# Strict mask by TensorE, forget rows on ScalarE, lambdas and copies of normed tiles as later steps, both ratios of a differential pair at once

## Time and profile before

| | us |
|---|---|
| median of three runs | 1549.19 |
| the profiled execution | 1553.94 |
| its span, first to last instruction | 1552.0 |
| TensorE busy | 1423.3 (92%) |
| VectorE busy | 904.6 (58%) |
| ScalarE busy | 681.2 (44%) |
| GpSimd busy | 366.7 (24%) |

### The profile page before, as it was taken

The page is one execution under the profiler, slowest core; times in us unless marked ns, Lnnn a source line. Parts: engine busy times, 40 slices in busy tenths (PEclk is TensorE's granted clock), DMA queues, the critical chain, the costliest instruction groups (busy, mean ns, idle before and its releaser), DMA issues.

```text
span 1552.0 us, 21224 instructions
## 1 busy us (share of the span) xinstructions
PE 1423.3 (92%) x8026; PEld 1097.0 (71%) x8026; DVE 904.6 (58%) x1705; ACT 681.2 (44%) x1477; POOL 366.7 (24%) x265
## 2 busy tenths in 40 slices
PE   7999898999989999999998699997999799997997
PEld 7757675877987576767788666665777656664776
DVE  4655437556672554484576565468655466568655
ACT  3544344555233554444552344335444444335443
POOL 2232121245231321222452111410001111310011
PEclk9999999999999999999999799999999899998999
DMA  6412620225333121211263323511213322511211
GB/s 225 109 29 85 158 68 28 62 61 204 109 136 82 29 82 55 82 35 56 67 224 85 93 54 68 116 55 48 93 64 96 82 63 60 116 55 48 96 62 54
DMA packets 191120, 131.72 MB, mean 85 GB/s; under 512 B 91436, under 2 KB 181164, under 8 KB 191020
## 3 DMA queue, kind: packets, MB, share of 16 engines
q1 hardware_dynamic: 179534, 112.29, 26.0%
q10 hardware_dynamic: 11486, 18.09, 3.6%
HBM read 118.03 MB, written 12.32 MB: 84 GB/s over the span
## 4 chain that ended last, share of the span: by engine, by line
PE 68%; DVE 18%; ACT 7%; issue 3%; DMA 2%; ACTq 1%; POOL 0%; DVEq 0%; POOLq 0%
PE pb L1399 18%; PE pb L1400 16%; PE pb L1401 16%; PE pb L1477 5%; PE pb L1421 5%; PE pb L1455 4%; ACT prob L1533 2%; DMA wr<-w_out 2%; ACT wh L1552 2%; ACT tmp L1533 1%; DVE wl L1861 1%; DVE scr L2151 1%; DVE xl L1868 1%; DVE small L2128 1%; PE pb L1439 1%
## 5 line engine op out<-in xcount | busy, mean ns | idle before, releaser
L2296 POOL TENSOR_TENSOR wl<-wr,wh 128x512 fp32r<-128x512 f32 x170 | 236.7, 1392 | 893.8 <-ACT wh L1552 890.1
L1399 PE MATMUL pb<-xh,wl 128*128 128x512 f32 (+1 forms) x832 | 354.0, 425 | 25.1 <-DVE xl L1868 21.9
L1400 PE MATMUL pb<-xl,wh 128*128 128x512 f32 (+1 forms) x832 | 323.6, 389 | 0.0
L1401 PE MATMUL pb<-xh,wh 128*128 128x512 f32 (+1 forms) x832 | 323.2, 388 | 0.0
L1861 DVE TENSOR_TENSOR wl<-wr,wh 128x512 fp32r<-128x512 f32 x200 | 162.9, 815 | 159.3 <-ACT wh L1552 159.0
L1399 PEld LDWEIGHTS pb<-xh,wl 128*128 128x128 f32 x832 | 164.0, 197 | 106.4 <-issue 54.1
L1552 ACT CAST wh<-wr 128x512 fp32r<-128x512 f32 x370 | 211.0, 603 | 50.2 <-PE pb L1401 42.8
L1401 PEld LDWEIGHTS pb<-xh,wh 128*128 128x128 f32 x832 | 163.5, 197 | 32.0
L1400 PEld LDWEIGHTS pb<-xl,wh 128*128 128x128 f32 x832 | 164.8, 198 | 24.3 <-issue 3.8
L1533 ACT ACTIVATE prob<-prob,small 128x512 f32<-128x512 f32 (+3 forms) x128 | 76.2, 597 | 153.0 <-DVE small L2105 143.6
L1455 PE MATMUL pb<-cst,prob 128*128 128x128 f32 x768 | 118.5, 276 | 24.4 <-ACT prob L1533 8.2
(11 more groups left out here) (196 smaller groups left out, 2449.9 us busy)
## 6 DMA issues: line engine op xcount, KB each, us to landing
wr<-w_in SPq DMA_DIRECT2D x39, 1024.0 KB, 5.1
wr<-w_in SPq DMA_DIRECT2D x48, 256.0 KB, 4.6
wr<-w_out SPq DMA_DIRECT2D x10, 1024.0 KB, 5.7
wr<-w_branch SPq DMA_DIRECT2D x48, 128.0 KB, 2.3
x<-prob SPq DMA_DIRECT2D x12, 512.0 KB, 2.6
wr<-w_out SPq DMA_DIRECT2D x48, 128.0 KB, 3.0
wr<-w_mem_kv SPq DMA_DIRECT2D x4, 1024.0 KB, 5.5
prob<-x ACTq DMA_DIRECT2D x2, 2048.0 KB, 10.3
```

The costliest lines, as they stand in the source:

```text
L1399: e.matmul(ps, ll, rh, start=start, stop=False)
L1400: e.matmul(ps, lh, rl, start=False, stop=False)
L1401: t = e.matmul(ps, lh, rh, start=False, stop=stop)
L2296: t = e.tensor_tensor(wl[:, j % 2, c0:c1], wr[:, j % 2, c0:c1], wh[:, j % 2, c0:c1].bitcast(F32), ALU.subtract)
```

## The change

1. The constant `after` (zeros and ones) becomes `strict` (0 and -1e30, 128 columns). `lambdas` also copies it and the identity to two new tiles. `sqk` adds per half one TensorE product of identity and mask to the diagonal block of the logits, after both halves' logits; both halves' logits are marked ready only then. `sticks` loses line 2154 and the mask in its scan.
2. `lambdas` and `spread` stand after the query projection of `sb` instead of before it.
3. `foxrow` is done by ScalarE (`Identity` with scale and bias) instead of VectorE.
4. `normed` keeps only the VectorE part. A step `normhi` with the ScalarE copies and the GpSimd differences is put when the planner's clock is 5000 further, or at the latest where `rest_of` is called: for the queries' group that is directly after `krope`, for the other group in the gate projection that follows.
5. `dmix` does reciprocal and product for both halves in one instruction each, after waiting for both halves' exponentials.

```diff
-    put("after", np.concatenate([np.zeros((P, 384)), c >= p], 1))
+    put("strict", np.where(c >= p, NEG, 0.0))
...
             put("normed", l=l, b=b, tm=tm, tn=tn, dim=dim, grp=grp, gain=gain)
             give(b, tm, tn)
+            ready = now() + 5000
+            for _ in range(40):
+                if now() < ready:
+                    yield
+            put("normhi", l=l, grp=grp)
...
         put("krope", l=l, b=b)
         give(b)
+        rest_of(norm_q)
...
+        rest_of(norm_kv)
         w = wnext("qb")
...
             yield from gate_into(box, "g1", "sb", l)
+            yield from proj_fm("sbq", l, "sb", "q", l, False)
             if l == 0:
                 put("lambdas")
                 put("spread")
-            yield from proj_fm("sbq", l, "sb", "q", l, False)
...
-                    t = e.matmul(bank(b)[:, 0:128 * (hi - lo)], lhs, rhs, start=True, stop=br != "mla")
-                    if br != "mla":
+                    t = e.matmul(bank(b)[:, 0:128 * (hi - lo)], lhs, rhs, start=True, stop=br not in ("mla", "sb"))
+                    if br not in ("mla", "sb"):
+                        t.then_inc(logit.sem, logit.mark(b))
+                if br == "sb":
+                    w.wait_ge(v_fn, v_fn.at("masks"))
+                    for b in s["b"]:
+                        t = e.matmul(bank(b)[:, 128 * i:128 * i + 128], identr[:, :], strict[:, :], start=False, stop=True)
                         t.then_inc(logit.sem, logit.mark(b))
...
-            elif k == "normed":
+            elif k == "normhi":
                 for n in s["grp"]:
                     w.wait_ge(v_fn, v_fn.at(("normed", s["l"], n)))
...
+            elif k == "foxrow":   # in scalar_program, out of vector_program
+                l, h = s["l"], s["h"]
+                w.wait_ge(v_fn, v_fn.at(("foxsum", l)))
+                w.wait_ge(p_fn, p_fn.at(("zeros", l)))
+                fa, fb = CONST_COLS["foxa"][0], CONST_COLS["foxb"][0]
+                p0 = 64 * (1 - h % 2)
+                for dst, n in ((QKV["fox"][0], 0), (QKV["fox"][1], 1 + h)):
+                    t = act(dst[p0:p0 + 36, h, :], fz[:, :], ACT.Identity, cst[0:36, fa + n:fa + n + 1],
+                            cst[0:36, fb + n:fb + n + 1])
+                    t.then_inc(a_copy.sem, a_copy.mark(("foxrow", l, h)))
...
             elif k == "lambdas":
+                w.wait_ge(d_tail, d_tail.at("tail"))
+                e.tensor_copy(identr[:, :], C("ident")).then_inc(v_fn.sem, v_fn.mark())
+                e.tensor_copy(strict[:, :], C("strict")).then_inc(v_fn.sem, v_fn.mark("masks"))
...
             elif k == "dmix":
                 l, i = s["l"], s["i"]
+                first, ratio = (small[:, s["sm"].slot.i, c + i:c + i + 5:4] for c in (8, 24))
+                for use in s["ta"]:
+                    w.wait_ge(a_att, a_att.at(("exp", use)))
+                e.reciprocal(ratio, ratio).then_inc(v_att.sem, v_att.mark())
+                w.wait_ge(v_att, v_att.n)
+                t = e.scalar_tensor_tensor(ratio, ratio, lam[:, l:l + 1], first, ALU.mult, ALU.mult)
+                t.then_inc(v_att.sem, v_att.mark())
+                w.wait_ge(v_att, v_att.n)
                 for half in range(2):
...
-                    m = mask_cols("after", 512 - n, 512)
-                    t = e.tensor_tensor_scan(lo[:, ::-1], x[:, ::-1], m[:, ::-1], 1.0, ALU.mult, ALU.max)
+                    t = e.tensor_tensor_scan(lo[:, ::-1], x[:, ::-1], x[:, ::-1], 1.0, ALU.mult, ALU.bypass)
...
-                    t = e.scalar_tensor_tensor(d[:, dg], mask_cols("after", 384, 512), 1.0, d[:, dg], ALU.is_lt, ALU.mult)
-                    t.then_inc(v_att.sem, v_att.mark())
...
-            elif k == "normed":   # in gpsimd_program
+            elif k == "normhi":
                 l = s["l"]
                 for n in s["grp"]:
                     own()
```

More of the change, by code:

```diff
@@ L1129, in build @@
     fz = sb("fz", [36, S])
+    identr, strict = sb("identr", [P, P], F32R), sb("strict", [P, P], F32R)
     mrh, mrl = sb("mrh", [P, S], F32R), sb("mrl", [P, S], F32R)
@@ L1335, in heads_ready @@
                 if br == "fox":
-                    w.wait_ge(v_fn, v_fn.at(("foxrow", l, 3)))
+                    w.wait_ge(a_copy, a_copy.at(("foxrow", l, 3)))
                 w.wait_ge(v_copy, v_copy.at(("value", l, br, 2)))
@@ L2012, in vector_program @@
                 t.then_inc(v_fn.sem, v_fn.mark(("foxsum", l), ends=(s["e"],)))
[L2013 to L2022, removed]
             elif k == "mergeup":
@@ L2131, in vector_program @@
                 l, i = s["l"], s["i"]
-                for half in range(2):
[L2133 to L2138, removed]
-                    t.then_inc(v_att.sem, v_att.mark())
-                    w.wait_ge(v_att, v_att.n)
-                    t = e.scalar_tensor_tensor(d, tm(use), ratio, d, ALU.mult, ALU.add)
+                first, ratio = (small[:, s["sm"].slot.i, c + i:c + i + 5:4] for c in (8, 24))
[6 more added lines that the diff above has]
+                w.wait_ge(v_att, v_att.n)
+                for half in range(2):
+                    d, p, use = probs(s["e"][half]), s["e"][half], s["ta"][half]
+                    t = e.scalar_tensor_tensor(d, tm(use), sm(s["sm"], 24 + 4 * half + i), d, ALU.mult, ALU.add)
                     t.then_inc(v_att.sem, v_att.mark(("mixed", p), ends=(use,)))
@@ L2146, in vector_program @@
                     w.wait_ge(d_spread, d_spread.at("z"))
-                    x, lo, d, dg = tm(use)[:, 0:n], tmpz[:, 0:n], probs(p)[:, 0:n], slice(n - 128, n)
+                    x, lo, d = tm(use)[:, 0:n], tmpz[:, 0:n], probs(p)[:, 0:n]
                     w.wait_ge(a_att, a_att.at(("keep", use)))
                     w.wait_ge(v_att, v_att.n)
-                    m = mask_cols("after", 512 - n, 512)
-                    t = e.tensor_tensor_scan(lo[:, ::-1], x[:, ::-1], m[:, ::-1], 1.0, ALU.mult, ALU.max)
+                    t = e.tensor_tensor_scan(lo[:, ::-1], x[:, ::-1], x[:, ::-1], 1.0, ALU.mult, ALU.bypass)
                     t.then_inc(v_att.sem, v_att.mark(ends=(use,)))
                     w.wait_ge(a_att, a_att.at(("break", p)))
-                    t = e.scalar_tensor_tensor(d[:, dg], mask_cols("after", 384, 512), 1.0, d[:, dg], ALU.is_lt, ALU.mult)
-                    t.then_inc(v_att.sem, v_att.mark())
                     w.wait_ge(v_att, v_att.n)
```

## The result

The changed kernel takes 1539.18 us (median of 4 runs, 1536.47 to 1541.01) against 1549.34 of before, run on the same chips: ratio 0.9928, 95% interval 0.9911 to 0.9946, so 11 us faster by the ratio and 10.2 by the medians. A second set of 6 runs gave 1539.16 and 0.9937 [0.9918, 0.9956]. The forecast was 1532 (1520 to 1543): the direction and the range held, but the gain is about 10 us and not 17.6.

What follows compares the result with a forecast made beforehand. It took TensorE, busy 92% of the span, as the bound; -10.1 (norms) + 0.2 (move) - 8.9 (stick breaking) + 3.0 (masks) - 1.8 (ratios) = -17.6 from 1549.2 gave 1531.6, predicted as 1532 us, range 1520 to 1543.

Steps and rivals of the forecast that it cites:

- clock terms: Matmuls behind shortened TensorE waits return to full clock: 4.3 us gained at the norms, 3.1 in stick breaking.
- Norms, gaps 5.8: Before `pv` in both layers: TensorE's waits of 3.12 and 3.07 fall to 0.2 each, 5.8 us gained.
- The port's 1.1: Second Newton step at the norms: GpSimd's differences may hold VectorE by 1.1 us per layer; in the range only.
- Move +0.2: `lambdas` and `spread`: ScalarE's blockade only moves, TensorE stands 5.9 us instead of 5.25; sum +0.2.
- Stick breaking, gaps 5.8: VectorE loses masks and `foxrow`, so four TensorE waits per layer shorten: 2.9 us per layer, 5.8 in all.
- the chain scan, clear, product loses its middle, 0.30: VectorE in stick breaking: removing the clear between scan and product shortens the path by 0.30 us each time.
- Masks +3.0: TensorE's 32 added mask products cost 2.2 us after hiding, plus 0.8 for changes of format: +3.0.
- ScalarE's `foxrow` 0: ScalarE's 16 added instructions, 11.6 us, fit into its pauses: cost 0, bounds 0 and +4.
- Rival D: In `sb`, `Identity` for `foxrow` forces function table loads between sigmoids, making the kernel slower: 1576 us; chance 0.03.
- Ratios -1.8: Branch D, `dmix`: joining both halves saves 0.44 us ahead of the waits of 3.51 and 3.09, both layers: -1.8.
- rival A: TensorE's waits shrink but the lower clock stays or falls elsewhere: 1539 us; chance 0.22 together with B.
- B: At the norms, something else becomes what `pv` waits for: 1539 us; chance 0.22 together with rival A.

Runs made afterwards that it cites:

- Mask and forget rows together: Kernel before with the strict mask added by TensorE and `foxrow` done by ScalarE, no other edit: 1546.55 us, ratio 0.9976.
- Norms alone: Kernel before with only the copies and differences of the normed tiles as a later step (`normhi`): 1540.17 us, ratio 0.9944.
- The kernel before with SyncE: Kernel before with the two DMAs of `spread` issued by SyncE instead of ScalarE, at the old place: 1542.64 us, ratio 0.9948.
- forget rows alone: Kernel before with only `foxrow` moved from VectorE to ScalarE: 1545.96 us, ratio 0.9969.
- ratios alone: Kernel before with only `dmix` doing reciprocal and product for both halves at once: 1550.30 us, ratio 1.0000.
- with SyncE: Changed kernel with the two DMAs of `spread` issued by SyncE instead of ScalarE: 1530.43 us, ratio 0.9880 to the kernel before.
- without masks: Changed kernel with SyncE issuing the DMAs of `spread` and VectorE masking the logits as before: 1528.62 us, ratio 0.9853 to the kernel before.

## Why the prediction was right, and where its size was not

**The gap terms held.** Without its clock terms (4.3 for the norms, 3.1 for stick breaking) the sum was -17.6 + 7.4 = -10.2. At equal clock the runs show 9.1 to 10.4. That it fits so well is in part luck, as the terms below were off by up to 1.2 us either way: the traces give 7.0 for the norms, 5.1 for stick breaking, 1.2 for the wait for GpSimd that had no term, 1.0 for the ratios, less 3.5 for the products and 0.5 for the move, together 10.3.

- *Norms, gaps 5.8:* the waits are gone entirely (rest forecast 0.2 each), and a wait of 0.73 before the transposes at 106.67, and its twin in layer 1, fell to 0.32, which no term had: 6.2 + 0.8 = 7.0 in the traces, 5.7 measured at equal clock for this edit alone. The port's 1.1, kept for the range, came as 0.8 and 1.0 (1.50 for 0.67, 1.66 for 0.69) and was hidden.
- *Move +0.2:* the new wait was forecast as 5.9 and is 5.75, ended by ScalarE's copy as said, at 183 and not 190. Measured +1.2 [-1.4, +3.9].
- *Stick breaking, gaps 5.8:* waits of 0.9, 0.7, 0.7, 0.7 were forecast, and are 0.81, 0.91, 0.88, 0.82. They sum to 3.42 per layer for 3.0, so 5.1 in all. The step that failed a little is "the chain scan, clear, product loses its middle, 0.30". The rows below (before, then after) show it: the clear had run in the time that the product must wait for the scan anyway. From one scan to its product it was 0.90, and without the clear it is 0.79: 0.11 is saved, and the wait before 235.23 fell by just that, 1.02 to 0.91. The first wait fell by 0.47, but 0.36 of it is time in which TensorE now computes the pair of mask products instead of standing, and so no gain.

```profile
232.33 0.68 DVE L2151 TENSOR_TENSOR_SCAN scr<-tmp,cst 128x256 f32<-128x256 f32 x1
232.93 0.27 DVE L2154 SCALAR_TENSOR_TENSOR prob<-cst,prob 128x128 f32<-128x128 f32 x1
233.23 0.42 DVE L2157 TENSOR_TENSOR prob<-prob,scr 128x255 f32<-128x255 f32 x1
```
```profile
225.05 0.68 DVE L2167 TENSOR_TENSOR_SCAN scr<-tmp 128x256 f32<-128x256 f32 x1
225.84 0.42 DVE L2171 TENSOR_TENSOR prob<-prob,scr 128x255 f32<-128x255 f32 x1
```

- *Masks +3.0:* 0.22 per step for 16 steps, 3.5 before what is hidden. The products that fall into waits show as shorter waits above, so the whole 3.5 counts here. Mask and forget rows together are 5.1 + 1.2 - 3.5 = 2.8; measured 3.7 [1.1, 6.2] with 0.7 of clock.
- *ScalarE's `foxrow` 0:* 12.2 us of work and no wait behind it. Rival D is out: no table load. The Trainium skill, ScalarE: Activation LUTs, section on table sets, has identity in every set; the rows agree.
- *Ratios -1.8:* waits fell by 1.1 alone and 1.0 in the whole. Per layer the 0.44 comes twice, as forecast, but not both times where forecast. The 3.51 gives 0.45. The `dmix` ahead of the 3.09 gives its 0.44 in the shorter wait before it, which the prediction did not name, and the 3.09 keeps its length: from the start of the logits ahead of both it is 1084.01 - 1078.53 = 5.48 before and 1067.32 - 1062.28 = 5.04 after. So it is not the later half's exponentials that keep the 3.09, as had been expected; the reciprocal of that `dmix` doesn't wait. They take back elsewhere: in four of the eight `dmix` of a layer the reciprocal stands about 0.53 for them, more than the 0.44 saved, once just ahead of the wait that grew from 0.20 to 0.48. Measured 0.0 [-2.2, +2.0].

**The clock terms failed.** The steps "the matmuls of 116 to 121 lose 1.85", "the other `pv` gives back 0.9", "the logits of 259.71 lose 0.75, and those behind them 0.5" are each true of the two traces: those stretches do run at full clock in the changed kernel. What failed is adding them to the time, as if a slow stretch belonged to its wait. The traces show that it doesn't. Norms alone has the waits of 2.35 and 2.36 with the logits at 0.92 and 1.65. The kernel before with SyncE has 2.38 and 2.36, and 0.92 both times. And with forget rows alone and with ratios alone the `pv` of layer 1 takes 1.08 behind a wait of 3.12, and the slow stretch begins only with the matmuls after it. In the changed kernel a new slow stretch stands behind the shorter waits of stick breaking in layer 1 (0.70 of full in 635 to 640), where before had none. The mean clock over the runs rose by 0.0009 only, 0.8 us for the 7.4 forecast. Norms alone had 0.0034, 3 us of the 4.3, so most of the term came for that edit and was given back in the whole; the stretches show where in the traces, 275 to 500 and 820 to 930, at waits of 4.26 and 7.19 that both kernels have. This is rival A, with its own price: 1539, and 1539.2 came. The reason that it gave, that what is left of the waits still brings the lower level, or that it falls elsewhere, is what the traces show; that the number came to 0.2 is in part luck, as above. That it is A and not B the waits decide: B's would stand before the `pv`, and nothing does.

By the table the single edits sum to -8.7 + 1.2 - 3.7 + 0.0 = -11.2, and the whole is -9.8 to -11.2: the parts add up to the whole within their intervals.

**What is not settled.** Why the clock that the norms bring back is lost elsewhere when masks, forget rows, ratios and the move come with them, and is there again with SyncE (+4.7, and +7.9 without masks). What sets the wait for GpSimd, and why either masks or forget rows take it away, is open too. The means rest on 5 to 12 runs each, with single runs from 0.969 to 0.975 for one kernel, so a difference of 0.0025 is near what they can tell. No experiment held the clock fixed.

## What to carry to other kernels

Price a wait and the low clock behind it apart, and trust the first: where a wait goes its length is gained, but slow stretches come back at the next long wait, so their sum over the span, and not their disappearance at one place, is the gain; read it from several executions. A blockade that is moved is still a blockade: give the issue of a long DMA to an engine that has nothing else to do. And before work goes from a lagging engine to the one that bounds the kernel, look at what else of the lagging engine's load can go to a third: here `foxrow` to ScalarE paid 4.8 us and the masks to TensorE nothing that can be told from none.

## What the runs showed of the hardware

- The issue of two DMAs (1920 KB each) held ScalarE for 9.5 us and SyncE for 10.95; only the issuing engine stands.
- Products of 128x128 by 128 columns in fp32r, behind float32 logits: 0.37 for two, or 0.26 for the first and 0.11 for each of three more, and the next fp32r matmul 0.28 instead of 0.43. The change of format is paid once.
- Taking an instruction out of a chain on VectorE saved 0.11 of its 0.30, since it had stood in the time between two others, of which the second waits for the first's result (0.79 from scan to product, not 0.60).
- The slow stretch behind a wait of TensorE is not tied to it: behind 2.35 and 2.36 in one execution the same logits took 0.92 and 1.65.
- The time of one and the same kernel scatters over 15 us (before: 1542.5 at a clock of 0.976, 1557.1 at 0.965), and the mean clock accounts for about three quarters of its variance.
